# The first product of a compression MLP: blocks as the stationary operand, or the weights

## The chip, the cores and the metric

The kernel runs on one core of a Trainium2 chip. The metric is the time of one execution on the device in microseconds (us). The engines are TensorE (PE in the rows, with its weight loads as PEld), VectorE (DVE), ScalarE (ACT), GpSimd (POOL) and SyncE (SP, which issues DMAs). Each has its own queue and waits on semaphores.

## The reference, cut to what matters

The model has a first block of two layers and a second block of two layers, on 256 tokens of width 1024. The change sits in the second block, in the branch with block-compressed attention. There the keys and the values of two groups are cut into 15 overlapping blocks of 32 tokens, and a small MLP turns every block into one key or value:

```python
NC = 15                                      # blocks of 32 tokens, 16 apart; G = 2 groups, hd = 64
blocks = concatenate([t_s[:, j:j + NC] for j in range(2)], axis=2) + pos_emb
flat = blocks.reshape(B, NC, G, 32 * 64)
return jax.nn.gelu(flat @ w1) @ w2           # w1: 2048 x 256, w2: 256 x 64

k_cmp = _compress(kc, pos_k, wk1, wk2)
v_cmp = _compress(vc, pos_v, wv1, wv2)
s_cmp = einsum('bsghd,bcgd->bghsc', q, k_cmp)     # scores against the 15 compressed keys
```

So the first product is, for keys and for values each, a 30 x 2048 matrix (2 groups x 15 blocks) times a 2048 x 256 one. Two other kinds of attention, over selected and over windowed keys, need nothing of it.

## The kernel before, in words

`second_layers` runs the two layers of the second block in one loop. Each engine has its program written out by hand, and semaphores (`E("name")`) tie them together. `PJ` and `TP` are pairs of PSUM banks that are used in a fixed order of named uses: `fill` waits until the bank's use before last was emptied, `full` marks it filled.

The attention is a loop over k with 12 groups (`GROUPS2`): groups 0 to 3 over selected keys, 4 to 7 over windowed keys, 8 to 11 over compressed keys. The first two of each four have 128 keys, the others 256; the compressed ones 128. In step k TensorE does the scores of group k (`scores`, L1276), then a share of the compression's first product (`compress`, L1238), then the transposes of the probabilities of group k-1 (`turn_p`, L1286) and the products with the values of group k-2 (`values`, L1297). VectorE adds the mask and takes the maximum of group k (L1702, L1902), scales the output of group k-2 (`output`, L1804 to L1816), and after it does one further piece of work from a table `with_group`: `keys_normalised` in step 3 (a reciprocal, L1859), `gelu_in` in step 5, `gelu_out` in step 6. ScalarE does the exponentials (L1587) and the copies out of PSUM (L1582). The scores of a group wait until VectorE has read those of the group before (`sc_read`).

`compress` works through 32 pieces of the contraction, 16 for keys and 16 for values, 7 in each of the steps 0 to 3 and 4 in step 4. A piece is one product: `BLK` (128 x 30, one column per block) stands in the array, and 256 columns of weights stream past it, from the slots `W.raw` into which they were loaded. The result has the 30 blocks on partitions. `gelu_in` copies it out and works on 30 x 512 elements, ScalarE takes the sigmoid (L1573), `gelu_out` multiplies. In step 7, ahead of the scores, TensorE turns the result by four transposes (`hidden`, L1249), VectorE copies it into `HID` (L1823), and `compressed` (L1257, L1262) makes the second product.

All this is in fp32. A product in fp32 leaves two records in the profile, a transpose one: 7 products are x14 in its rows.

Of the kernel before, what the change touches and what calls it, by code (L numbers as in the profile page):

```python
# [6 lines left out]
P = 128  # L7
# [970 lines left out]
def second_layers(nc, chip, A, layers=DEPTH):  # L978
    ctx = Scope()
    with ctx:  # L980
# [32 lines left out]


        HID = H[:, :, RV:RV + HALF].rearrange("p k (f n) -> p k f n", f=2)
        ge = [KP[:, 0:2, :], KP[:, 2:4, :], BP[:, :, :]]
        kcT = H[:, 0, 0:S].rearrange("p (g n) -> p g n", g=2)
        vcp = H[:, 1, 0:P].rearrange("p (g n) -> p g n", g=2)
        part_out = H[:, 0, S:2 * S]
# [83 lines left out]

        tp = [("x", i) for i in range(4)] + [("f", i) for i in range(9)] + [("mv",), ("mw",), ("ma",), ("mg",), ("mz",)]
        tp += [("q", i) for i in range(2)] + [("d", i) for i in range(4)] + [("kn",)]
        tp += [("o", a) for a in range(5)] + [("hd",), ("kc",), ("vc",)]
        tp += [("o", a) for a in range(5, len(GROUPS2))]
        tp += [("bn",), ("kp", 0), ("kp", 1), ("ba", 0), ("ba", 1), ("vt",), ("W",), ("Q",)]
        tp += [("n", 0), ("n", 1)] + [(k, i) for i in range(2) for k in ("U", "I", "D")] + [("Y", 0)]
# [17 lines left out]
        def E(name):  # L1127
            if name not in ev:
                ev[name] = Count(ctx, nc, "e_" + name)
            return ev[name]  # L1130
# [14 lines left out]
        with nc.Fori(0, layers) as l:  # L1145
          with nc.Block() as block:
# [16 lines left out]
            def _(pe):  # L1163
# [65 lines left out]
                def compress(kv, i):  # L1229
                    s = ("cmp", kv)  # L1230
                    b = PJ.fill(pe, (s, 0)) if i == 0 else PJ.aps[PJ.at[(s, 0)] % 2]
                    if i == 0:
                        pe.wait_ge(E("blk").sem, kv + 1)
                    item = W.first[s] + i // 4
                    if i % 4 == 0:
                        W.wait_landed(pe, item)
                    slot = W.raw(item).rearrange("p c (i f) -> p (c i) f", i=2)
                    ins = pe.matmul(b[0:2 * NC, 0:S], BLK[:, kv, i, :], slot[:, i % 4, :], start=(i == 0), stop=(i == 15))  # L1238
                    if i in (3, 7, 11):
                        ins.then_inc(W.used.sem, 1)  # L1240
                    if i == 15:
                        PJ.full(ins)

                def hidden():

                    b = TP.fill(pe, ("hd",))
                    pe.wait_ge(E("gelu").sem, 1)
                    for n in range(4):
                        ins = pe.transpose(b[:, n * 2 * NC:(n + 1) * 2 * NC], ge[0][0:2 * NC, n // 2, (n % 2) * P:(n % 2) * P + P],  # L1249
                                           chip.ident[0:2 * NC, 0:2 * NC])  # L1250
                    TP.full(ins)

                def compressed():
                    b = TP.fill(pe, ("kc",))
                    TP.taken(pe, ("hd",))
                    for f in range(2):
                        ins = pe.matmul(b[:, 0:2 * P], w2k[:, f, :], HID[:, 0, f, :], start=(f == 0), stop=(f == 1))  # L1257
                    TP.full(ins)
                    b = TP.fill(pe, ("vc",))
                    for g in range(2):  # L1260
                        for f in range(2):
                            ins = pe.matmul(b[:, g * HD:(g + 1) * HD], HID[:, 1, f, g * P:(g + 1) * P], w2v[:, f, :],  # L1262
                                            start=(f == 0), stop=(f == 1))
                    TP.full(ins)
# [38 lines left out]
                for k in range(G + 2):  # L1303
                    if k == 2:
                        b = TP.fill(pe, ("kn",))
                        pe.wait_ge(E("ksq").sem, 1)
                        TP.full(pe.matmul(b[:, :], chip.ones[:], TM2.rearrange("p c s -> p (c s)"), start=True, stop=True))
                    if k == 7:
                        hidden()
                    if k < G:  # L1310
                        scores(k)
                    for n in range(7 * k, min(7 * k + 7, 32)):
                        compress(n // 16, n % 16)
                    if 0 <= k - 1 < G:
                        turn_p(k - 1)
                    if k == 7:
                        compressed()
                    if 0 <= k - 2 < G:
                        values(k - 2)
# [175 lines left out]
            def _(act):  # L1495
# [65 lines left out]
                for a in range(G + 1):  # L1561
                    if a == 0:

                        act.wait_ge(E("cum").sem, 1)
                        lane.done(sc.activation(EP[:, :, :], CUM[:, :, :], ACT.Exp), E("exps"))
                        lane.done(sc.activation(EE[:, :, :], EE[:, :, :], ACT.Exp), E("exps"))
                    if a == 1:
                        lane.done(sc.activation(EN[:, :, :], CUM[:, 2:4, :], ACT.Exp, scale=-1.0), E("exps"))
                        lane.done(sc.activation(EM[:, :, :], EM[:, :, :], ACT.Exp), E("exps"))
                    if a == 6:  # L1570

                        act.wait_ge(E("ge_in").sem, 1)
                        lane.done(sc.activation(ge[2][0:2 * NC], ge[1][0:2 * NC], ACT.Sigmoid, scale=2.0 * 0.7978845608028654), E("ge_sig"))  # L1573
                    if a == 2:
                        b = TP.read(act, ("kn",))
                        TP.empty(lane, sc.activation(TM, both(b), ACT.Sqrt), ("kn",))
                    if a >= 1:
                        act.wait_ge(E("pt_full").sem, a)
                        if a - 1 >= 2:
                            act.wait_ge(TP.filled.sem, TP.at[("o", a - 3)] + 1)  # L1580
                        n = keys(a - 1) // P
                        lane.done(sc.copy(PT[:, (a - 1) % 2, 0:n, :], ptb[:, 0:n, :]), E("pt"))  # L1582
                    if a < G:
                        act.wait_ge(E("mx").sem, a + 1)
                        for s in range(4):
                            p = sm[:, a % 2, s, 0:keys(a)]
                            lane.done(sc.activation(p, p, ACT.Exp, bias=nmx[:, a, s:s + 1], accum_out=den[:, a, s:s + 1]),  # L1587
                                      E("p") if s == 3 else None)
# [95 lines left out]
            def _(dve):  # L1684
# [132 lines left out]

                Kn, Rn = FT[:, F_K:F_K + 2, :], FT[:, F_R:F_R + 2, :]

                def hidden():  # L1820
                    b = TP.read(dve, ("hd",))
                    for kv in range(2):
                        ins = v.tensor_copy(HID[:, kv, :, :].rearrange("p f (g n) -> p f g n", g=2)[:, :, :, 0:NC],  # L1823
                                            b[:, kv * 4 * NC:(kv + 1) * 4 * NC].rearrange("p (f g n) -> p f g n", f=2, g=2))
                        lane.done(ins) if kv == 0 else TP.empty(lane, ins, ("hd",))

                def compressed():
                    b = TP.read(dve, ("kc",))
                    TP.empty(lane, v.tensor_copy(H[:, 0, 0:S], b[:, 0:2 * P]), ("kc",))
# [8 lines left out]
                    stt(Kn, BB[:, :, :], 1.0, Kn, ALU.add, ALU.mult)  # L1838


                blocks = slice(0, 2 * NC)

                def gelu_in():
                    for kv in range(2):
                        b = PJ.read(dve, (("cmp", kv), 0))
                        PJ.empty(lane, v.tensor_copy(ge[0][blocks, kv, :], b[blocks, 0:S]), (("cmp", kv), 0))
                    tt(ge[1][blocks], ge[0][blocks], ge[0][blocks], ALU.mult)
                    ts(ge[1][blocks], ge[1][blocks], 0.044715, 1.0, ALU.mult, ALU.add)
                    tt(ge[1][blocks], ge[1][blocks], ge[0][blocks], ALU.mult, E("ge_in"))

                def gelu_out():
                    dve.wait_ge(E("ge_sig").sem, 1)
                    tt(ge[0][blocks], ge[0][blocks], ge[2][blocks], ALU.mult, E("gelu"))

                def keys_normalised():
                    TP.drained(dve, ("kn",))
# [29 lines left out]
                G = len(GROUPS2)  # L1886
                dve.wait_ge(E("gate").sem, 1)
                for k in range(G + 2):
                    if k == 7:
                        hidden()  # L1890
                    if k < G:
                        kind, t, g = GROUPS2[k]
                        nk = keys(k)
                        dve.wait_ge(E("sc_full").sem, k + 1)
                        if k >= 2:

                            dve.wait_ge(E("pt_full").sem, k - 1)
                        p = sm[:, k % 2, :, 0:nk]
                        bias = (chip.cmpb if kind == "c" else chip.cbias)[:, t, 0:nk].unsqueeze(1).to_broadcast([P, 4, nk])
                        stt(p, scb[:, :, 0:nk], 0.125, bias, ALU.mult, ALU.add, E("sc_read"))  # L1900
                        lane.settle()
                        lane.done(v.tensor_reduce(nmx[:, k, :], p, AX_X, ALU.max, negate=True), E("mx"))  # L1902
                    if k == 7:
                        compressed()
                    if k - 2 >= 0:
                        output(k - 2)
                    if k in with_group:
                        with_group[k]()
# [322 lines left out]
```

## Time and profile before

| | us |
|---|---|
| median of three runs | 1833.7 |
| lowest and highest run | 1832.84, 1835.09 |
| span of the profiled execution (first to last instruction) | 1835.8 |
| TensorE busy in it, weight loads aside | 1599.5 |
| VectorE, ScalarE, GpSimd busy | 785.5, 778.1, 968.8 |

The profiled execution is one more execution, apart from the three; of it the profile gives the span. The granted clock is the share of TensorE's full clock of 2.4 GHz that the chip allows; it has two levels, 1.00 and 0.50 (1.2 GHz), and a value between them is a mean over a stretch in which it changed. The steps of the attention stand in the profile at 864 to 950 us (first layer of the second block) and at 1403 to 1488 us (second).

### The profile page before, as it was taken

To read this page: it belongs to the slowest core of one execution; us is meant where nothing else is said; L and a number is where in the kernel's file an instruction comes from. 1 tells how busy PE (TensorE), PEld (TensorE's weight loads), DVE (VectorE), ACT (ScalarE), POOL (GpSimd) and SP (SyncE) were. 2 spreads that over 40 slices of the span, in tenths; PEclk is the share of its full clock that TensorE was granted. 3 is DMA by queue.
4 is the path that set the end of the run, shared out by engine and by line. 5 is a ranking of instruction groups with operands and counts; after the bars stand their busy time and mean duration, and the time that the engine had idled before them with its cause. 6 is when DMAs were issued, how large, how long until landed. Compare 5 with 4: busy or idle time off the path is not lost. (4 is left out here: it accounts for less than half of the span.)

```text
span 1835.8 us, 22140 instructions
## 1 busy us (share of the span) xinstructions
PE 1599.5 (87%) x8104; PEld 1309.1 (71%) x8104; DVE 785.5 (43%) x1135; ACT 778.1 (42%) x1233; POOL 968.8 (53%) x416
## 2 busy tenths in 40 slices
PE   5998999969989999797878789999797868889997
PEld 3876787758867877575568668887575658767885
DVE  5106853541068535108676461111127685551112
ACT  4443664334436643355531234443355522234442
POOL 4785457748854587472000339877670000358875
PEclk8999999989999999797868889999798869789999
DMA  5564335445633354551200326654651100336553
GB/s 165 160 199 121 92 110 160 155 123 162 195 115 92 113 164 146 174 174 51 92 1 1 115 69 190 181 163 144 184 155 61 58 1 22 94 104 193 167 179 125
DMA packets 120671, 228.17 MB, mean 124 GB/s; under 512 B 9968, under 2 KB 22896, under 8 KB 120560
## 3 DMA queue, kind: packets, MB, share of 16 engines
q1 hardware_dynamic: 119408, 222.51, 40.9%
q10 hardware_dynamic: 1152, 4.19, 0.8%
q8 instruction: 68, 1.11, 0.3%
q14 instruction: 43, 0.35, 0.1%
HBM read 225.63 MB, written 1.05 MB: 123 GB/s over the span
## 5 line engine op out<-in xcount | busy, mean ns | idle before, releaser
L162 POOL TENSOR_TENSOR parts<-raw,parts 128x1024 fp32r<-128x1024 f32 (+4 forms) x412 | 968.6, 2362 | 848.6 <-ACT parts L155 846.6
L193 PE MATMUL ps<-parts,xT 128*128 128x512 f32 (+3 forms) x2624 | 812.3, 390 | 24.3 <-ACT xT L1645 7.0
L155 ACT CAST parts<-raw 128x1024 fp32r<-128x1024 f32 (+4 forms) x412 | 417.1, 1015 | 506.7 <-PE ps L193 277.7
L193 PEld LDWEIGHTS ps<-parts,xT 128*128 128x128 f32 x2624 | 496.0, 192 | 134.0 <-ACT xT L1645 7.9
L193 PE MATMUL ps<-parts,x_low 128*128 128x512 f32 (+2 forms) x672 | 255.4, 389 | 0.0
L193 PE MATMUL ps<-parts,M_low 128*128 128x512 f32 (+2 forms) x640 | 244.9, 387 | 0.0
L193 PEld LDWEIGHTS ps<-parts,x_low 128*128 128x128 f32 x672 | 131.1, 195 | 25.2
L193 PEld LDWEIGHTS ps<-parts,M_low 128*128 128x128 f32 x640 | 120.9, 189 | 21.2
L193 PE MATMUL ps<-parts,aT 128*128 128x512 f32 x352 | 109.5, 394 | 0.0
L193 PE MATMUL ps<-parts,H_low 128*128 128x512 f32 x272 | 106.1, 395 | 0.0
L765 DVE TENSOR_TENSOR acc<-H,rope1s 128x512 f32<-128x512 f32 (+1 forms) x6 | 9.6, 1599 | 192.2 <-ACT H L646 192.1
L193 PEld LDWEIGHTS ps<-parts,aT 128*128 128x128 f32 x352 | 66.1, 188 | 15.8 <-POOL parts L162 0.4
L193 PE MATMUL ps<-parts,ysT 128*128 128x512 f32 x192 | 62.7, 399 | 4.9 <-DVE sm L896 4.9
L193 PE MATMUL ps<-parts,mn_high 128*128 128x512 f32 x128 | 47.1, 444 | 21.7 <-ACT parts L155 17.8
L1691 DVE TENSOR_TENSOR DL<-FT 128x2550 f32<-128x2550 f32 x2 | 5.6, 2815 | 128.3 <-ACT FT L1522 128.3
L2098 DVE TENSOR_TENSOR EE<-ps,EE 128x512 f32<-128x512 f32 (+1 forms) x24 | 15.4, 647 | 104.1 <-ACT EE L1671 104.1
L193 PEld LDWEIGHTS ps<-parts,H_low 128*128 128x128 f32 x272 | 51.1, 188 | 11.7
L1362 PE MATMUL ps<-arena 128*128 128x128 f32 x448 | 55.1, 290 | 4.4 <-DVE arena L1967 4.4
L1362 PEld LDWEIGHTS ps<-arena 128*128 128x128 f32 x448 | 54.8, 205 | 5.0 <-DVE arena L1691 5.0
L2105 DVE TENSOR_TENSOR H<-ps,EE 128x512 f32<-128x512 f32 (+1 forms) x24 | 15.5, 647 | 96.7 <-PE ps L193 96.7
L2051 DVE SCALAR_TENSOR_TENSOR x<-x,ps 128x512 f32<-128x512 f32 x16 | 10.9, 682 | 105.5 <-PE ps L193 105.4
L1587 ACT ACTIVATE arena<-arena,nmx 128x128 f32<-128x128 f32 (+1 forms) x96 | 40.7, 426 | 28.4 <-DVE nmx L1902 28.4
(310 smaller groups left out, 2003.5 us busy)
## 6 DMA issues: line engine op xcount, KB each, us to landing
raw<-in_w_in SPq DMA_DIRECT2D x168, 512.0 KB, 3.6
raw<-in_ffn_w_down SPq DMA_DIRECT2D x44, 512.0 KB, 4.2
raw<-in_ffn_w_gate SPq DMA_DIRECT2D x40, 512.0 KB, 3.8
raw<-in_ffn_w_up SPq DMA_DIRECT2D x40, 512.0 KB, 4.4
raw<-in_w_out SPq DMA_DIRECT2D x32, 512.0 KB, 3.8
raw<-in_w_branch SPq DMA_DIRECT2D x24, 512.0 KB, 4.3
raw<-in_w_mem_kv SPq DMA_DIRECT2D x16, 512.0 KB, 3.9
raw<-in_w_in SPq DMA_DIRECT2D x16, 366.0 KB, 3.2
```

Source lines behind the costliest of these rows:

```text
L155: self.nc.scalar.copy(self.part(i, 0)[:, 0:nk, 0:w], self.raw(i)[:, 0:nk, 0:w]).then_inc(self.hi_ready.sem, 1)
L162: self.nc.gpsimd.tensor_tensor(self.part(i, 1)[:, 0:nk, 0:w], self.raw(i)[:, 0:nk, 0:w], self.part(i, 0)[:, 0:nk, 0:w], ALU.subtract).then ...
L193: ins = pe.matmul(b[:, 0:w], a(k0 + 2 * n + c, t), self.part(i, lo_w)[:, c, 0:w], start=(opens and n == p == 0), stop=(final and p == len( ...
L765: lane.done(v.tensor_tensor(a_, X[:, :, :, 0:16], C.unsqueeze(2).to_broadcast([P, NT, nh, 16]), ALU.mult))
L1362: ins = pe.matmul(b[:, u, :], L[:, 4 * par + u, :], R[:, 4 * par + u, :], start=True, stop=True)
L1587: lane.done(sc.activation(p, p, ACT.Exp, bias=nmx[:, a, s:s + 1], accum_out=den[:, a, s:s + 1]), E("p") if s == 3 else None)
L1691: lane.done(v.tensor_tensor(out, a, b, op), e)
L2051: banks.empty(lane, v.scalar_tensor_tensor(out=xs, in0=xs, scalar=ALPHA, in1=b[:, :], op0=ALU.mult, op1=ALU.add), ((s, j), t))
L2098: PJ.empty(lane, v.tensor_tensor(sg[:, t, 0:w], b[:, 0:w], sg[:, t, 0:w], ALU.mult), (("gt", j), t))
L2105: ins = v.tensor_tensor(H[:, t, c0:c0 + w], b[:, 0:w], sg[:, t, 0:w], ALU.mult)
```

## The change: what it does

The weights are now the stationary operand and the blocks stream. A piece takes two products, one for each half of the 256 features: 128 x 128 weights stand, 30 columns of `BLK` stream. The result comes out with the features on partitions, 60 columns for keys and 60 for values. The four transposes and the two copies of `hidden` are gone, with their use ("hd",) of `TP`; `gelu_in`, the sigmoid and `gelu_out` work on 128 x 120 elements in place of 30 x 512, and `gelu_out` writes `HID` itself, in two instructions.

```diff
-        ge = [KP[:, 0:2, :], KP[:, 2:4, :], BP[:, :, :]]
+        ge = [u[:, 0, 0:8 * NC].rearrange("p (k n) -> p k n", k=2) for u in (KP, KP[:, 2:4], BP)]
...
-                    ins = pe.matmul(b[0:2 * NC, 0:S], BLK[:, kv, i, :], slot[:, i % 4, :], start=(i == 0), stop=(i == 15))
+                    for f in range(2):
+                        ins = pe.matmul(b[:, f * 2 * NC:(f + 1) * 2 * NC], slot[:, i % 4, f * P:(f + 1) * P], BLK[:, kv, i, :],
+                                        start=(i == f == 0), stop=(i == 15 and f == 1))
...
-                def hidden():
-
-                    b = TP.fill(pe, ("hd",))
-                    pe.wait_ge(E("gelu").sem, 1)
-                    for n in range(4):
-                        ins = pe.transpose(b[:, n * 2 * NC:(n + 1) * 2 * NC], ge[0][0:2 * NC, n // 2, (n % 2) * P:(n % 2) * P + P],
-                                           chip.ident[0:2 * NC, 0:2 * NC])
-                    TP.full(ins)
-
                 def compressed():
                     b = TP.fill(pe, ("kc",))
-                    TP.taken(pe, ("hd",))
+                    pe.wait_ge(E("gelu").sem, 2)
...
-                    if k == 7:
-                        hidden()
...
                 def gelu_out():
                     dve.wait_ge(E("ge_sig").sem, 1)
-                    tt(ge[0][blocks], ge[0][blocks], ge[2][blocks], ALU.mult, E("gelu"))
+                    for kv in range(2):
+                        tt(HID[:, kv, :, :].rearrange("p f (g n) -> p f g n", g=2)[:, :, :, 0:NC],
+                           ge[0][:, kv, :].rearrange("p (f g n) -> p f g n", f=2, g=2),
+                           ge[2][:, kv, :].rearrange("p (f g n) -> p f g n", f=2, g=2), ALU.mult, E("gelu"))
```

TensorE's order at the start of the loop, steps 0 to 2, before (an "x7" here is 7 products, 14 records of the profile):

```order
L1276 MATMUL ps<-arena 128x128 x4
L1238 MATMUL ps<-raw,arena 30x256 x7
L1276 MATMUL ps<-arena 128x128 x4
L1238 MATMUL ps<-raw,arena 30x256 x7
L1286 MATMUL ps<-ident,arena 128x128 x4
L1307 MATMUL ps<-DL,ones 128x512
L1276 MATMUL ps<-arena 128x256 x4
```

The same place now (L1239 is the compression's product, L1269 the scores, L1279 the transposes):

```order
L1269 MATMUL ps<-arena 128x128 x4
L1239 MATMUL ps<-arena,raw 128x30 x14
L1269 MATMUL ps<-arena 128x128 x4
L1239 MATMUL ps<-arena,raw 128x30 x14
L1279 MATMUL ps<-ident,arena 128x128 x4
L1300 MATMUL ps<-DL,ones 128x512
L1269 MATMUL ps<-arena 128x256 x4
```

Each run of 7 products with 256 streaming columns has become one of 14 with 30; the work around it stands as it did.

TensorE's order in steps 6 and 7 before, from the scores of group 6 to the second product:

```order
L1276 MATMUL ps<-arena 128x256 x4
L1286 MATMUL ps<-ident,arena 128x128 x4
L1297 MATMUL ps<-H,arena 128x64 x4
L1249 MATMUL ps<-ident,DL 128x30 x4
L1276 MATMUL ps<-arena 128x256 x4
L1286 MATMUL ps<-ident,arena 128x128 x8
L1257 MATMUL ps<-H,w2k 128x256 x2
L1262 MATMUL ps<-w2v,H 128x64 x4
```

The same place now (L1290 is the product with the values, L1250 and L1255 the second product):

```order
L1269 MATMUL ps<-arena 128x256 x4
L1279 MATMUL ps<-ident,arena 128x128 x4
L1290 MATMUL ps<-H,arena 128x64 x4
L1269 MATMUL ps<-arena 128x256 x4
L1279 MATMUL ps<-ident,arena 128x128 x8
L1250 MATMUL ps<-H,w2k 128x256 x2
L1255 MATMUL ps<-w2v,H 128x64 x4
```

The four transposes ahead of the scores of group 7 are gone; the wait for the activated result has moved behind the transposes of group 6.

## Rows read from the trace of the kernel before

**Rows 1.** The page: time, TensorE's busy time, granted clock in 40 slices.

```profile
span 1835.8 us, 22140 instructions
...
PE 1599.5 (87%) x8104; PEld 1309.1 (71%) x8104; DVE 785.5 (43%) x1135; ACT 778.1 (42%) x1233; POOL 968.8 (53%) x416
...
PEclk8999999989999999797868889999798869789999
```

**Rows 2.** Chain that ended last, second layer: start us, us, what.

```profile
1416.04 3.14 PE ps L1238 x14
...
1433.79 3.36 DVE DL L1859
```

**Rows 3.** Timeline of TensorE, first layer, steps 0 to 7: start us, us busy.

```profile
870.53 5.65 PE L1238 MATMUL ps<-raw,arena 128*30 128x256 f32 x14 [4.93 <-issue]
876.11 0.71 PE L1276 MATMUL ps<-arena 64*128 64x128 f32 x8
...
880.39 1.02 PE L1307 MATMUL ps<-DL,ones 128*128 128x512 f32 x2
881.34 1.13 PE L1276 MATMUL ps<-arena 64*128 64x256 f32 x8
...
893.04 0.71 PE L1276 MATMUL ps<-arena 64*128 64x128 f32 x8
...
914.04 0.60 PE L1249 MATMUL ps<-ident,DL 30*128 30x30 f32 x4 [4.02 <-DVE DL L1691]
```

**Rows 4.** Stretches: us, busy us (instructions) of PE, PEld, DVE, ACT, POOL, PEclk, DMA, GB/s.

```profile
870.53:875.50 4.97, 4.97 (x12) 2.08 (x13) 3.52 (x6) 1.08 (x6) 0.00 (x0) 0.50 0.06 11
...
876.10:893.10 17.00, 17.00 (x103) 10.10 (x102) 8.25 (x12) 9.75 (x24) 0.00 (x0) 1.00 0.56 178
...
1052.50:1060.00 7.50, 7.50 (x34) 7.28 (x34) 3.69 (x9) 2.07 (x3) 0.00 (x0) 0.50 0.02 3
```

**Rows 5.** Groups of TensorE's instructions in 1052.5 to 1060 us.

```profile
L1420 PE MATMUL ps<-H,arena 128*128 128x64 f32 x8 | 2.5, 421 | 0.0
```

**Rows 6.** Timeline of TensorE, second layer, steps 4 to 9.

```profile
1438.75 1.23 PE L1276 MATMUL ps<-arena 64*128 64x128 f32 x8 [1.18 <-DVE arena L1702]
1441.15 1.11 PE L1286 MATMUL ps<-ident,arena 128*128 128x128 f32 x4 [1.18 <-ACT arena L1587]
1442.06 3.52 PE L1297 MATMUL ps<-H,arena 128*128 128x64 f32 x16
1445.50 2.08 PE L1276 MATMUL ps<-arena 64*128 64x256 f32 x8
...
1454.58 2.08 PE L1276 MATMUL ps<-arena 64*128 64x256 f32 x8
1456.59 1.97 PE L1286 MATMUL ps<-ident,arena 128*128 128x128 f32 x8
1458.35 1.46 PE L1257 MATMUL ps<-H,w2k 128*128 128x256 f32 x4
...
1463.05 1.90 PE L1297 MATMUL ps<-H,arena 128*128 128x64 f32 x16
1464.88 0.72 PE L1276 MATMUL ps<-H,arena 64*128 64x128 f32 x8
```

**Rows 7.** Timeline of VectorE, first layer, steps 4 to 7.

```profile
900.34 0.18 DVE L1804 RECIPROCAL fac<-den 128x4 f32<-128x4 f32 x1
...
906.35 0.73 DVE L1846 COPY DL<-ps 30x256 f32<-30x256 f32 x2
...
909.20 1.23 DVE L1702 SCALAR_TENSOR_TENSOR arena<-ps,cbias 128x1024 f32<-128x1024 f32 x1
...
913.21 0.68 DVE L1691 TENSOR_TENSOR DL<-DL,BP 30x512 f32<-30x512 f32 x1
914.68 0.35 DVE L1823 COPY H<-ps 128x60 f32<-128x60 f32 x2 [0.79 <-PE ps L1249]
916.70 1.22 DVE L1702 SCALAR_TENSOR_TENSOR arena<-ps,cbias 128x1024 f32<-128x1024 f32 x1 [1.67 <-PE ps L1276]
```

More of the change, by code:

```diff
@@ L1105, in second_layers @@
         tp += [("q", i) for i in range(2)] + [("d", i) for i in range(4)] + [("kn",)]
-        tp += [("o", a) for a in range(5)] + [("hd",), ("kc",), ("vc",)]
+        tp += [("o", a) for a in range(5)] + [("kc",), ("vc",)]
         tp += [("o", a) for a in range(5, len(GROUPS2))]
@@ L1572, in _ @@
                         act.wait_ge(E("ge_in").sem, 1)
-                        lane.done(sc.activation(ge[2][0:2 * NC], ge[1][0:2 * NC], ACT.Sigmoid, scale=2.0 * 0.7978845608028654), E("ge_sig"))
+                        lane.done(sc.activation(ge[2], ge[1], ACT.Sigmoid, scale=2.0 * 0.7978845608028654), E("ge_sig"))
                     if a == 2:
@@ L1818, in _ @@
                 Kn, Rn = FT[:, F_K:F_K + 2, :], FT[:, F_R:F_R + 2, :]
[L1820 to L1825, printed above, removed]
                 def compressed():
@@ L1838, in keys_mixed @@
                     stt(Kn, BB[:, :, :], 1.0, Kn, ALU.add, ALU.mult)
-                blocks = slice(0, 2 * NC)
                 def gelu_in():
@@ L1845, in gelu_in @@
                         b = PJ.read(dve, (("cmp", kv), 0))
[L1846 to L1849, printed above, removed]
+                        PJ.empty(lane, v.tensor_copy(ge[0][:, kv, :], b[:, 0:4 * NC]), (("cmp", kv), 0))
+                    tt(ge[1], ge[0], ge[0], ALU.mult)
+                    ts(ge[1], ge[1], 0.044715, 1.0, ALU.mult, ALU.add)
+                    tt(ge[1], ge[1], ge[0], ALU.mult, E("ge_in"))
                 def gelu_out():
                     dve.wait_ge(E("ge_sig").sem, 1)
-                    tt(ge[0][blocks], ge[0][blocks], ge[2][blocks], ALU.mult, E("gelu"))
+                    for kv in range(2):
+                        tt(HID[:, kv, :, :].rearrange("p f (g n) -> p f g n", g=2)[:, :, :, 0:NC],
+                           ge[0][:, kv, :].rearrange("p (f g n) -> p f g n", f=2, g=2),
+                           ge[2][:, kv, :].rearrange("p (f g n) -> p f g n", f=2, g=2), ALU.mult, E("gelu"))
                 def keys_normalised():
@@ L1888, in _ @@
                 for k in range(G + 2):
-                    if k == 7:
-                        hidden()
                     if k < G:
```

## The prediction

> **What bounds the kernel now.** I read the page first. TensorE is busy for 1599.5 us of the span, and in the slices around 870 to 950 us and 1400 to 1490 us its granted clock dips [rows 1]. These are the attention steps of the two layers, the only place that the change touches. The chain that ended last says what the end waits for there: in steps 0 to 3 it stays on TensorE, with the 14 records of a share of the compression as its largest piece, 3.14 us, and in step 4 it passes over to VectorE at the reciprocal of 3.36 us [rows 2]. From there to the end of the loop it goes through the cycle of mask, exponential, transposes and values. So steps 0 to 3 are worth what TensorE takes for them, and later steps are worth the waits between engines.
>
> The timeline of TensorE gives the lengths. The compression's first share starts at 870.53, the scores of group 1 at 876.11, and the scores of group 4, the end of step 3, at 893.04, with no gap [rows 3]. The stretches give the clock: 0.50 from 870.5 to 875.5, then 1.00 for the whole of 876.1 to 893.1, with TensorE busy for 17.00 of 17.00 us [rows 4]. Before the rise TensorE had done twelve records with 256 streaming columns. That clock of 1.00 is the thing to watch: every piece in steps 1 to 4 is short because of it.
>
> **The change part by part.**
>
> *The compression's product.* 64 records per layer with 256 streaming columns become 128 with 30 columns, each with 128 columns of weights to load. The trace has no product with 30 streaming columns. The nearest is the values' product: 128 columns loaded, 64 streaming. At the full clock 16 of its records take 1464.88 - 1463.05 = 1.83 us, 0.114 each; at 0.50, 1445.50 - 1442.06 = 3.44 us, 0.215 each [rows 6]. A record with 256 columns takes 3.14 / 14 = 0.224 at the full clock [rows 2], so a stream of 64 columns should take a quarter, 0.056. The record costs twice that: the weight load sets it, and fewer columns make it no cheaper. I take 0.114 and 0.215. A share of 28 records is then 3.20 us at the full clock (before 3.14) and 6.02 at 0.50 (before 5.58, which included the first records after the rise) [rows 2, 3]. The other bound is that load and stream lie one after the other: 0.114 = 0.058 + 0.056, and 30 columns would make 0.058 + 0.026 = 0.084, or 0.16 at 0.50. That would take 0.03 x 128 = 3.8 us per layer off at the full clock, 7 us at 0.50.
>
> So at equal clock the product costs the same as before. The multiplications fall out of it, the loads come in.
>
> *The clock.* This decides. Where TensorE worked through records of 128 loaded and 64 streaming columns it did not get its full clock however busy it was: from 1052.5 to 1060 us it was busy for 7.50 of 7.50 us, and the clock stood at 0.50 throughout [rows 4]; 24 of the 34 records there are of three such lines, 8 each, of which one row is shown [rows 5]. The 3.44 us of the values at 1442.06 are such a stretch too, and the scores behind them still run slowly (2.01 us) [rows 6]. The new shares stream half as many columns per load. In step 0 the engine starts at 0.50, so nothing there should lift it, and in steps 1 to 4 they are the largest piece. I take 0.50 for steps 0 to 4.
>
> The price of the other pieces at 0.50: scores with 128 keys 1.2 us (busy time 1.23), with 256 keys 1456.59 - 1454.58 = 2.01; four transposes 1442.06 - 1441.15 = 0.91, eight 1458.35 - 1456.59 = 1.76; values with 16 records 3.44, so 1.72 with 8 [rows 6]; the product with `ones` twice 881.34 - 880.39, 1.9 [rows 3].
>
> - step 0: compression 6.0
> - step 1: 1.2 + 6.0 + 0.9 = 8.1
> - step 2: 1.9 + 2.0 + 6.0 + 0.9 + 1.7 = 12.5
> - step 3: 2.0 + 6.0 + 1.8 + 1.7 = 11.5
>
> Together 38.1 us in place of 893.04 - 870.53 = 22.5: **+15.6 us**. In step 4 TensorE then needs 1.2 + 3.4 (16 records) + 1.8 + 3.4 = 9.8 us until the values of group 2 are there, at about 918.5. VectorE took up their output at 900.34 [rows 7], held by the reciprocal, which hid TensorE's step; at 0.50 it no longer does. The delay grows to about **+18.2 us**. Steps 5 to 7 are at 0.50 before as well, mostly, and carry it on.
>
> *What is given back.* `gelu_in` took 909.20 - 906.35 = 2.85 us on 512 elements per partition. A copy of 60 takes 0.35 / 2 = 0.18 [rows 7]; with two such copies and three operations on 120 at about 0.3 with their waits, it takes some 1.5: **-1.3**. From `gelu_out` to the mask of group 7 VectorE took 916.70 - 913.21 = 3.49 us [rows 7]: the multiplication, the wait for TensorE's transposes, the copies, and the wait for the scores of group 7, which stood behind them, while TensorE idled 4.02 us for the result [rows 3]. Now the scores of group 7 are done in this idle time and VectorE goes on after two products of 60 elements, some 0.5 us: **-3.0**. The wait for the activated result moves behind the transposes of group 6. Behind it are queued the second product and the values of group 5, for which VectorE waits; `gelu_out` is done about when the exponentials of group 6 are, so it adds nothing. The shorter sigmoid is a part of ScalarE's waiting. The second product is unchanged.
>
> Per layer: 18.2 - 4.3 = +13.9 us with the clock at 0.50 throughout. It may rise in between, where `ones`, 256-key scores and transposes stand together. These pieces of steps 2 and 3 are 6.5 + 5.5 = 12 us at 0.50; all of them at 1.00 would save 6, and a share that followed at 1.00 another 2.8. I take 1.5 off, as a choice between 0 and 9. So +12.4 per layer, **+25 for two**: the profiled execution of 1835.8 becomes 1861, and the median, 2.1 below it, **1858**.
>
> A rule speaks against this sum. The Trainium skill (TensorE: Matmul & The Clock Gate, section "Why this matters for your kernels") asks for one thing for the full rate, that TensorE is kept busy without a break; by that the new shares would raise the clock as the old did. The trace contradicts it at 1052.5 to 1060 us, busy throughout at 0.50 [rows 4].
>
> **The rivals.**
>
> *The clock rises all the same and stays up: faster.* The place is the end of step 0. For it speaks that TensorE is busy without a gap in steps 0 to 3, as before, and that the full clock, once there, survives 1.83 us of values records in a row [rows 6]. Against it: 7.50 us at 0.50 [rows 4]. Then the shares cost 3.20 for 3.14, +0.3 us per layer with step 4, and the 4.3 us come back whole: -4.0 per layer, -8 in all, **1826**. It turns where the delay of steps 0 to 4 is under 4.3 us per layer, that is where TensorE is at 0.50 for less than some 9 of its 22 us after step 0. By the page's rule above it would come out like this.
>
> *The load is cheaper than I take it, the clock low.* By the other bound above, 7 us per layer less: +5.4 per layer, about **1845**.
>
> *The clock is not lifted anywhere and stays low in steps 8 to 11 as well*, which before ran partly at 1.00: some 5 us more per layer on top of the 13.9, **1871**.
>
> *Both effects cancel*: the clock is up for about half of steps 1 to 4, and the delay is about 4 us: **1834**, no change.
>
> **How the numbers follow.** The forecast, clock at 0.50 for most of steps 0 to 4, from +8 to +15 per layer (1850 to 1864), has 0.66. The cheaper load has 0.07, the clock low to the end 0.09, cancelling 0.04, and the clock up 0.14. The cases on the slow side sum to 0.82. The range leaves out the clock that stays up and the cancelling, 0.18: from 1838, a cheap load with some rises, to 1874, a little above the rival with the low clock. A measurement tells this kernel from no change at about 0.2%, 3.7 us: faster 0.14, within it 0.04, slower 0.82.
>
> **What the changed profile would show.** The granted clock in the stretches of steps 1 to 4: near 0.50 by the forecast, 1.00 by the first rival. A share of the compression as x28 in about 6.0 us, or 3.2. The time from its first record to the scores of group 4: 38 us, or 22.6. VectorE's output of group 2 waiting for TensorE. In step 7 no wait of 4 us ahead of the scores, and some 1.5 us for `gelu_in`. A record of the new product well under 0.114 at the full clock, or under 0.215 at half, would refute the load as its price. The forecast is wrong if the clock column stays at 1.00; nothing else in it is large enough to turn the sign.

## The result, and the profile after

The changed kernel takes 1852.25 us in the median of five runs (1844.17 to 1857.63), the kernel before 1833.7 in the median of five (1827.09 to 1837.12). The ratio is 1.0095, with an interval of 1.0068 to 1.0123: slower by some 18 us, where 25 were forecast. The profiled execution of the changed kernel has a span of 1848.1 us, 12.3 above that of before.

The page of the changed kernel, in the lines that answer to [rows 1], and one group of its part 5:

```profile
span 1848.1 us, 22374 instructions
...
PE 1626.6 (88%) x8224; PEld 1352.8 (73%) x8224; DVE 780.7 (42%) x1133; ACT 777.4 (42%) x1233; POOL 968.6 (52%) x416
...
PEclk9999999989999999797669789999896659889999
...
L1239 PE MATMUL ps<-arena,raw 128*128 128x30 f32 x256 | 50.9, 372 | 9.9 <-issue 9.9
```

TensorE's busy time is up by 27 us, and the clock is lower in the slices around 900 us and from 1390 to 1480 us. The busy time of the group is no measure of its cost, since records overlap; starts are. The timeline of TensorE in the second layer (start us, us busy), the answer to [rows 3]:

```profile
1410.80 6.15 PE L1239 MATMUL ps<-arena,raw 128*128 128x30 f32 x28 [4.93 <-issue]
1416.88 1.23 PE L1269 MATMUL ps<-arena 64*128 64x128 f32 x8
...
1428.77 6.18 PE L1239 MATMUL ps<-arena,raw 128*128 128x30 f32 x28
...
1448.87 1.23 PE L1269 MATMUL ps<-arena 64*128 64x128 f32 x8
...
1458.64 1.23 PE L1269 MATMUL ps<-arena 64*128 64x128 f32 x8
```

And in the first layer:

```profile
870.63 6.15 PE L1239 MATMUL ps<-arena,raw 128*128 128x30 f32 x28 [4.93 <-issue]
...
877.87 6.18 PE L1239 MATMUL ps<-arena,raw 128*128 128x30 f32 x28
883.86 1.09 PE L1279 MATMUL ps<-ident,arena 128*128 128x128 f32 x4
...
887.74 3.31 PE L1239 MATMUL ps<-arena,raw 128*128 128x30 f32 x28
890.89 0.64 PE L1279 MATMUL ps<-ident,arena 128*128 128x128 f32 x4
...
899.49 1.23 PE L1269 MATMUL ps<-arena 64*128 64x128 f32 x8
```

The same share of 28 records stands here at both prices: 883.86 - 877.87 = 5.99 us, and 890.89 - 887.74 = 3.15 us. Which one it gets is told by the stretches of the changed kernel (columns as in [rows 4]):

```profile
870.63:886.80 16.17, 16.17 (x72) 14.38 (x74) 6.12 (x11) 4.49 (x18) 0.00 (x0) 0.50 0.33 98
886.90:897.00 10.10, 10.10 (x89) 9.28 (x88) 5.66 (x7) 6.04 (x14) 0.00 (x0) 1.00 0.39 116
897.10:899.49 2.39, 2.39 (x13) 2.27 (x11) 0.00 (x0) 1.49 (x4) 0.00 (x0) 0.50 0.76 253
1410.80:1448.87 38.07, 38.07 (x170) 34.40 (x171) 11.77 (x18) 12.13 (x35) 0.00 (x0) 0.50 0.33 97
```

TensorE is busy without a pause in all four. In the second layer the clock is 0.50 for the whole of steps 0 to 3, which take 38.07 us. In the first layer it rises at 886.8 us, in the scores of group 2 right behind the product with `ones`, and stays up for 10 us; the same steps take 899.49 - 870.63 = 28.86 us.

VectorE in steps 5 to 7 of the first layer, the answer to [rows 7]:

```profile
915.64 0.34 DVE L1828 COPY DL<-ps 128x60 f32<-128x60 f32 x2
...
917.11 1.23 DVE L1693 SCALAR_TENSOR_TENSOR arena<-ps,cbias 128x1024 f32<-128x1024 f32 x1
...
921.12 0.47 DVE L1682 TENSOR_TENSOR H<-DL,BP 128x60 f32<-128x60 f32 x2
921.73 1.23 DVE L1693 SCALAR_TENSOR_TENSOR arena<-ps,cbias 128x1024 f32<-128x1024 f32 x1
```

`gelu_in` takes 1.47 us (2.85 before), and from `gelu_out` to the mask of group 7 there are 0.61 us (3.49 before).

### The profile page after: what moved, and what is told of

The parts are those of the page before. It is cut to its first block and busy times, and to the rows that moved or that the text cites. A ratio compares the mean times of both kernels' runs of the same rounds, so it can differ in the third digit from the quotient of the medians.

```text
span 1848.1 us, 22374 instructions
## 1 busy us (share of the span) xinstructions
PE 1626.6 (88%) x8224; PEld 1352.8 (73%) x8224; DVE 780.7 (42%) x1133; ACT 777.4 (42%) x1233; POOL 968.6 (52%) x416
## 5 line engine op out<-in xcount | busy, mean ns | idle before, releaser
L193 PE MATMUL ps<-parts,mn_high 128*128 128x512 f32 x128 | 47.1, 445 | 20.2 <-ACT parts L155 18.2
L1239 PE MATMUL ps<-arena,raw 128*128 128x30 f32 x256 | 50.9, 372 | 9.9 <-issue 9.9
L1239 PEld LDWEIGHTS ps<-arena,raw 128*128 128x128 f32 x256 | 49.7, 301 | 13.2 <-issue 13.2
```

The costliest lines, as they stand in the source:

```text
L193: ins = pe.matmul(b[:, 0:w], a(k0 + 2 * n + c, t), self.part(i, lo_w)[:, c, 0:w], start=(opens and n == p == 0), stop=(final and p == len( ...
L1239: ins = pe.matmul(b[:, f * 2 * NC:(f + 1) * 2 * NC], slot[:, i % 4, f * P:(f + 1) * P], BLK[:, kv, i, :], start=(i == f == 0), stop=(i == ...
```

## The experiments

All were timed against the kernel before on the same chip; e1 to e4, e5 to e8 and e9 to e11 had a chip per group, so between the groups the ratios are what compares. To compare profiles, the attention loop of each layer is measured from the first scores of group 0 to the product with `ones` behind the loop; before that is 945.96 - 864.38 = 81.58 us and 1485.62 - 1403.51 = 82.11. The whole execution also moves by what the clock does elsewhere: 29 runs of the kernel before lay between 1817.94 and 1842.21, and of the 17.3 us by which the span of e1 is below that of before, 8.1 lie in the two loops. A loop in this table is one profile's.

| kernel | median us | ratio (interval) | loop, layers one and two, against before |
|---|---|---|---|
| changed | 1852.25 | 1.0095 (1.0068 to 1.0123) | +3.8, +12.5 |
| changed, again (e4) | 1853.57 | 1.0110 (1.0071 to 1.0149) | +13.2, +12.7 |
| 120 columns (e1) | 1822.77 | 0.9953 (0.9929 to 0.9977) | -5.1, -3.0 |
| 60 columns (e2) | 1830.81 | 0.9985 (0.9962 to 1.0007) | +1.1, +1.5 |
| before, transposes moved (e3) | 1840.01 | 1.0030 (1.0009 to 1.0052) | +3.6, +2.7 |
| changed, warmed (e5) | 1840.39 | 1.0028 (1.0004 to 1.0052) | +7.7, +8.7 |
| 120 columns, warmed (e6) | 1821.01 | 0.9936 (0.9915 to 0.9957) | -3.9, -6.0 |
| 120 columns, early wait (e7) | 1821.63 | 0.9941 (0.9914 to 0.9968) | -2.8, -2.4 |
| before, warmed (e8) | 1832.41 | 0.9993 (0.9974 to 1.0012) | 0.0, -0.1 |
| 120 columns, values 128 (e9) | 1824.04 | 0.9939 (0.9918 to 0.9959) | -0.9, -3.8 |
| changed, values 128 (e10) | 1835.52 | 1.0019 (0.9999 to 1.0039) | +6.5, +3.1 |
| before, values 128 (e11) | 1833.00 | 0.9992 (0.9972 to 1.0013) | +0.3, -0.1 |

**More streaming columns behind the same loads (e1, e2).** With c = 4 or c = 2 copies of the 30 columns:

```diff
-                        ins = pe.matmul(b[:, f * 2 * NC:(f + 1) * 2 * NC], slot[:, i % 4, f * P:(f + 1) * P], BLK[:, kv, i, :],
-                                        start=(i == f == 0), stop=(i == 15 and f == 1))
+                        ins = pe.matmul(b[:, f * c * 2 * NC:(f + 1) * c * 2 * NC].rearrange("p (r n) -> p r n", r=c), slot[:, i % 4, f * P:(f + 1) * P],
+                                        BLK[:, kv, i, :].unsqueeze(1).to_broadcast([P, c, 2 * NC]), start=(i == f == 0), stop=(i == 15 and f == 1))
...
```

VectorE's copies in `gelu_in` read the first copy of the columns only.

> The changed kernel, but each of its 64 products streams the same 30 block columns four times over, 120 columns in all, into four places of the bank, of which one is read. Loads, number of records, everything behind them and the result stay as they are in the changed kernel; only the streaming columns per load change. Theory (the low clock in steps 0 to 4 is the loss, and it stands low because TensorE mostly loads): the clock rises after step 0 and stays at 1.00 through steps 1 to 4, a share of 28 records takes 3.2 us, and only what the change gives back remains: 4.0 us per layer under the kernel before, about 1826 us. Rival (the loss is in the records themselves, in loads that add to the stream or in their number): a record with four times the columns takes at least as long as now, 0.215 us, and the time is that of the changed kernel, 1852 us, or more.

> As the kernel with 120 streaming columns, but the 30 columns are streamed twice, 60 columns per load, which is the shape nearest to the values' product with its 64. Theory: stretches of such records stood at 0.50 in the kernel before (1052.5 to 1060 us), so the shares alone don't lift the clock, but the pieces between them do so more often than in the changed kernel: between the two, 1835 to 1850 us. Rival (the clock follows how long TensorE is busy, whatever it does): 1852 us, as changed. Rival (the records themselves): 1852 us or more.

With 120 columns the kernel takes 1822.77 us: 30 us less than the changed kernel, for streaming four times as much. The timeline of TensorE and a stretch of it:

```profile
870.34 3.38 PE L1239 MATMUL ps<-arena,raw 128*128 128x120 f32 x28
873.56 0.60 PE L1279 MATMUL ps<-ident,arena 128*128 128x128 f32 x4
...
886.70 0.72 PE L1269 MATMUL ps<-arena 64*128 64x128 f32 x8
```

```profile
868.60:886.70 18.10, 18.10 (x153) 16.22 (x151) 8.25 (x12) 11.18 (x32) 0.00 (x0) 1.00 0.58 176
```

A share takes 873.56 - 870.34 = 3.22 us, against 3.15 for 30 columns at the same clock, and the clock is 1.00 from the rise in step 0 to the end of step 3. The theory stands, and its rival, that the records themselves are the loss, falls: longer records, and a faster kernel. What remains is the give-back, -5.1 and -3.0 us in the loops, where -4.0 per layer was forecast.

With 60 columns I expected 1835 to 1850 and measured 1830.81. The timeline shows why this is better than expected:

```profile
869.93 6.20 PE L1239 MATMUL ps<-arena,raw 128*128 128x60 f32 x28 [4.93 <-issue]
...
877.22 6.23 PE L1239 MATMUL ps<-arena,raw 128*128 128x60 f32 x28
...
886.78 3.33 PE L1239 MATMUL ps<-arena,raw 128*128 128x60 f32 x28
889.95 0.61 PE L1279 MATMUL ps<-ident,arena 128*128 128x128 f32 x4
...
892.39 3.34 PE L1239 MATMUL ps<-arena,raw 128*128 128x60 f32 x28
```

Two shares in a row stay at the low clock, as the records of 64 columns did at 1052.5 to 1060 us [rows 4]. Then it rises, in the product with `ones` here (at some 885.4 us) and in the scores of group 2 in the other layer, and with these shares it stays; from 885.5 to 898 us it is 1.00. With shares of 30 columns it fell again in the changed kernel, at 897.0 us, after two of them. So a shape with which the clock does not rise can still be one with which it stays.

**The changed kernel a second time (e4).**

> The changed kernel once more, unaltered, for a second profile. In the first one the clock stood at 0.50 through steps 0 to 4 of the second layer, but rose from 886.8 to 897.1 us in the first, where the delay to the end of the loop was 3.8 us in place of 12.5. Theory (whether the clock rises between the shares hangs on how the pieces fall against the chip's own grid): the second profile has another pattern of rises, in either layer, and the runs spread over 1842 to 1860 us as before. Rival (the first layer has something of its own that lifts the clock, such as the transfers): the same pattern again, up in the first layer and low in the second.

The time is confirmed, 1853.57 us, and the pattern is another one: both layers at 0.50 through steps 0 to 3. The stretches:

```profile
868.40:906.38 37.98, 37.98 (x170) 34.31 (x170) 11.69 (x18) 12.13 (x35) 0.00 (x0) 0.50 0.32 96
1421.20:1459.30 38.10, 38.10 (x172) 34.43 (x172) 11.78 (x18) 12.16 (x35) 0.00 (x0) 0.50 0.32 97
```

The first layer's +3.8 us in the first profile is therefore no property of that layer. That execution had a rise between the shares, this one has none before step 4 (there, in the product with the values, the clock rises in both layers), and its span is 1860.9 us. What decides it I did not vary: that it hangs on how the pieces fall against a grid of the chip, as the expectation has it, stays an assumption.

**The order alone (e3).**

```diff
-                    if k == 7:
-                        hidden()
                     if k < G:
                         scores(k)
...
                     if k == 7:
+                        hidden()
                         compressed()
...
```

> The kernel before, with its product as it was, and only the four transposes of the MLP's result moved: from ahead of the scores of group 7 to behind the transposes of group 6, and VectorE's copies with them, to behind the mask and maximum of group 7. This is the part of the give-back that is order alone. Theory: scores and mask of group 7 no longer wait for the result; of the 3.0 us that the removal of the transposes gives in step 7, some 2 remain per layer, 1829 to 1831 us. Rival (the wait only moves, since the second product and the values of group 5 now stand behind it): 1833.7 us.

This went the other way, 0.3% slower, and neither theory had it. TensorE in steps 6 to 8:

```profile
914.69 1.97 PE L1286 MATMUL ps<-ident,arena 128*128 128x128 f32 x8 [2.23 <-ACT arena L1586]
916.59 0.63 PE L1249 MATMUL ps<-ident,DL 30*128 30x30 f32 x4
917.76 2.04 PE L1257 MATMUL ps<-H,w2k 128*128 128x256 f32 x4 [0.53 <-DVE H L1822]
919.60 1.80 PE L1262 MATMUL ps<-w2v,H 128*128 128x64 f32 x8
921.19 1.91 PE L1297 MATMUL ps<-H,arena 128*128 128x64 f32 x8
```

In the kernel before the same two pieces are:

```profile
916.58 1.97 PE L1286 MATMUL ps<-ident,arena 128*128 128x128 f32 x8
...
920.82 1.06 PE L1297 MATMUL ps<-H,arena 128*128 128x64 f32 x8
```

The loop starts at 863.94 us here and at 864.38 before. Counted from there, the transposes of group 6 start at 50.75 us, 1.4 earlier than before (52.20). Then the four transposes and a wait of 0.53 us for VectorE's copies stand on TensorE's path to the second product, and the second product and the values of group 5 run at the low clock: the values start at 57.25 us, before at 56.44. The pieces behind them stay slow to 927.3 us, where before the clock was up from 919.9. So the head start is more than used up. The changed kernel has the same order without transposes and copies. The profiled execution is the slowest of the twelve, so how much of the 0.3% each of the two makes is not shown.

**The wait put back (e7).** The kernel with 120 columns, and in step 7:

```diff
+                    if k == 7:
+                        pe.wait_ge(E("gelu").sem, 2)
                     if k < G:
                         scores(k)
```

> The kernel with 120 streaming columns, but in step 7 TensorE waits for the activated result ahead of the scores of group 7, where the four transposes stood before. Nothing else is changed. It undoes the order part of the give-back at a clock that is up. Theory (what step 7 gives back is the scores and the mask of group 7, freed of the wait): 1.5 to 2.5 us per layer are lost again, 1826 to 1828 us. Rival (the gain in step 7 comes from the missing transposes and copies, and the place of the wait is worth nothing, as the slower run with the transposes moved suggests): 1823 us.

The times do not tell it from e1 (1821.63 and 1822.77), and the loops are only 2.2 and 0.6 us longer; the 1826 to 1828 us that I expected did not come. VectorE shows the local price:

```profile
912.49 0.47 DVE L1684 TENSOR_TENSOR H<-DL,BP 128x60 f32<-128x60 f32 x2
914.73 1.22 DVE L1695 SCALAR_TENSOR_TENSOR arena<-ps,cbias 128x1024 f32<-128x1024 f32 x1 [1.77 <-PE ps L1269]
```

From `gelu_out` to the mask there are 2.24 us, against 3.49 before and 0.61 in the changed kernel. Of the 2.9 us that step 7 gives back, the place of the wait is 1.6 in this layer, and transposes, copies and the shorter multiplication are 1.3; in the other layer the split is 2.0 and 0.9. The scores behind the wait took 1.67 us in this layer, against 1.13 in the changed kernel, so the clock that was up in steps 1 to 4 was not up here. What the wait is worth in the time stays open, since it is less than a measurement tells.

**A raised clock to begin with (e5, e6, e8).** In step 0, ahead of the first share:

```diff
+                    if k == 0:
+                        for _ in range(5):
+                            pe.matmul(ptb[:, 0, :], chip.ones[:], chip.masks[:, 0:4, :].rearrange("p a n -> p (a n)"), start=True, stop=True)
```

> The changed kernel, and in the 4.9 us in which TensorE waits for the block columns in step 0 it does five idle products of 128 x 512 (constants, into a bank that is free), whose result nobody reads. They bring the full clock to the first share, and shares of 30 columns follow. Theory (shares of 30 streaming columns don't hold the full clock): part of share 0 runs at 1.00, some 2 to 3 us per layer less, then the clock falls again during share 0 or 1 and stands at 0.50 in most of steps 1 to 4; 1845 to 1851 us beside the changed kernel's 1853. Rival (a clock once up survives such records, as it did 1.83 us of values' products): 1.00 through steps 0 to 4, as with 120 columns and 3 us per layer better, 1817 us.

> The same five idle products, ahead of the shares with 120 streaming columns. Theory (step 0 runs at 0.50 only because TensorE stood idle before it, and its 6.0 us are on the path): share 0 takes 3.2 to 4.5 us in place of 6.0, 1.5 to 2.8 us per layer, so 1817 to 1820 us beside 1823 without them. Rival (what step 0 saves is lost again, since VectorE's masks and ScalarE's exponentials of group 0 then are what step 1 waits for): 1823 us.

> The kernel before with the five idle products ahead of its first share. Theory (as for 120 columns): share 0 drops from 5.6 to 3.1 to 4.2 us, 1.4 to 2.5 us per layer, 1829 to 1832 us. Rival: the clock falls earlier in steps 5 to 7 by as much as it rises earlier, no change against the kernel before.

In steps 0 and 1 e5 did what the theory says. Its timeline and stretches:

```profile
863.58 6.07 PE L1305 MATMUL ps<-masks,ones 128*128 128x512 f32 x10
869.49 3.21 PE L1239 MATMUL ps<-arena,raw 128*128 128x30 f32 x28
872.62 0.72 PE L1269 MATMUL ps<-arena 64*128 64x128 f32 x8
873.26 6.01 PE L1239 MATMUL ps<-arena,raw 128*128 128x30 f32 x28
...
883.80 3.31 PE L1239 MATMUL ps<-arena,raw 128*128 128x30 f32 x28
886.95 0.95 PE L1279 MATMUL ps<-ident,arena 128*128 128x128 f32 x4
```

```profile
869.49:873.40 3.91, 3.91 (x39) 3.75 (x37) 2.73 (x6) 0.86 (x5) 0.00 (x0) 1.00 0.24 46
873.60:883.60 10.00, 10.00 (x41) 7.90 (x40) 2.38 (x5) 4.99 (x16) 0.00 (x0) 0.50 0.42 138
```

Share 0 runs at 1.00 and takes 3.13 us; the clock then falls, with TensorE busy throughout, and share 1 takes 5.83. The rival, that a clock once up survives such records, is refuted. The time, 1840.39 us, is below the 1845 to 1851 that I expected, although the warming has a price that the expectations left out. The idle products take longer than the wait of 4.93 us, so share 0 starts 7.07 and 6.88 us behind the first scores in the two layers, in the changed kernel 6.15. At its end 2.0 and 2.2 us are left, 4.2 of the 13 by which e5 is faster. More came from share 2, which ran at 1.00 in both layers: 886.95 - 883.80 = 3.15 us, and 3.15 in the second, 2.8 less each than at 0.50. Whether the warm start brings these later rises, one profile does not tell.

At the full clock the warming gives little: 1821.01 against 1822.77 (e6) and a ratio of 0.9993 for the kernel before (e8), whose loops are as long as without it. Share 0 starts 1.0 to 1.5 us later there as well. In the first layer of e8 it still ends 1.2 us ahead of before; then the clock falls earlier (the transposes of group 4 take 1.11 us, before 0.66), and the scores of group 8 start at 57.40 us from the first scores, before at 57.43. So e8 went to its rival.

**The same trick on the values' product (e9, e10, e11).**

```diff
-                            ins = pe.matmul(b[:, s * HD:(s + 1) * HD], PT[:, a % 2, kt, s * P:(s + 1) * P], v,
+                            ins = pe.matmul(b[:, s * P:(s + 1) * P].rearrange("p (r d) -> p r d", r=2), PT[:, a % 2, kt, s * P:(s + 1) * P],
+                                            v.unsqueeze(1).to_broadcast([P, 2, HD]),
```

> The kernel with 120 streaming columns in the compression, and the same done to the values' product of the attention loop: its 64 columns are streamed twice, 128 per load, into twice as many columns of the bank, of which VectorE reads the first copy. The result is the same. Theory (a record that loads 128 columns costs its load, 0.114 us at the full clock, up to 128 streaming columns, and what streams behind the load keeps the clock up): values' records at 1.00 take no longer, and the clock is up in more of steps 4 to 11, 1 to 3 us per layer less: 1816 to 1821 us beside 1822.8. Rival (in steps 5 to 11 TensorE idles for VectorE and ScalarE, and the clock there follows the pauses): no change, 1823 us. Rival (the record gets longer by its stream): slower than 1823.

> The changed kernel, 30 streaming columns in the compression, with only the values' 64 columns streamed twice. It asks whether the pieces between the shares lift the clock enough. Theory: steps 2 to 4 have rises more often, since the values' records stream as many columns as they load; 1838 to 1848 us beside 1853. Rival (the shares alone decide): 1853 us.

> The kernel before with only the values' 64 columns streamed twice. Theory: steps 0 to 4 have the full clock already, so only steps 4 to 11 can gain, 1 to 3 us per layer: 1828 to 1832 us. Rival (pauses decide there): 1834 us. If this gains as much as it does on top of the kernel with 120 columns, the two effects add.

On the changed kernel it takes 18 us off (1835.52 for 1853.57; by the ratios, 17), more than the 5 to 15 expected, although the compression is untouched. On the kernel with 120 columns and on the one before it gives nothing, where 1 to 3 us per layer were expected: 1824.04 and a ratio of 0.9992. There steps 1 to 4 have the full clock already, and the rival is what the times agree with. Where the 18 us of e10 arise its profile tells in part only. TensorE in the second layer:

```profile
1422.61 1.62 PE L1269 MATMUL ps<-arena 64*128 64x256 f32 x8
...
1428.44 1.92 PE L1290 MATMUL ps<-H,arena 128*128 128x128 f32 x8
1430.28 1.20 PE L1269 MATMUL ps<-arena 64*128 64x256 f32 x8
```

The clock rises first at 1423.5 us, in the scores of group 2 and so ahead of the loop's first product with the values, as it did in the changed kernel; it falls, rises again at 1430.3 right behind that product, and then stays at 1.00 to 1448. In the first layer it stood at 0.50 to 894.5 us and was at 1.00 from 901.5 to 942.3, so part of the gain lies behind the shares. That the pieces between the thin shares count for the clock is shown by the time; that they bring the rises in steps 0 to 3 is not.

## Why the prediction was right, and where it was off

*What bounds it.* Steps 0 to 3 are worth what TensorE takes for them. Right: every stretch of them above is filled, and where the delay was +18.7 at step 4 the loop still ended 12.5 later.

*The price of a record.* Forecast 0.114 and 0.215 us. Measured 3.15 / 28 = 0.1125 and 5.99 / 28 = 0.214. The other bound, load and stream one after the other, 0.084, is refuted twice: by 30 columns, and by 120, whose share takes 3.22 us (0.115 per record). At equal clock the product costs what it cost before, as said.

*The clock.* The decisive step, right: steps 0 to 3 took 38.07 us at 0.50 in three of four layers profiled (in e4 the stretches are cut at 37.98 and 38.10), where the sum gave 38.1. That the low clock is the loss, and not only beside it, is shown by e1: the same loads, the same number of records, the clock at 1.00, and the loss gone.

*The rises in between.* Here the sum was mis-sized: "I take 1.5 off, as a choice between 0 and 9". One layer of four took off 38.1 - 28.86 = 9.2, the other three nothing. With +18.6 in the medians instead of the 27.8 at 0.50 throughout, they are worth about 4.6 us per layer in the mean, if all the rest is as forecast, and 3.5 with the +12.8 us per layer that the layers without a rise in steps 0 to 3 measured. The two profiles show a layer either with a rise worth 9 us or with none, not a small saving in each; of the other runs there is no trace. That 1852 came so near to 1858 is in part luck, since the 1.5 was a choice.

*The delay at step 4.* Forecast +18.2. In the second layer the scores of group 5, which before waited 1.18 us for VectorE and now do not wait, start 1458.64 - 1410.80 = 47.8 us behind the first share, before 1438.75 - 1409.66 = 29.1: +18.7. In e4, where the clock rose in step 4, it was +18.1 and +18.0. The line of before that [rows 6] does not have:

```profile
1409.66 5.74 PE L1238 MATMUL ps<-raw,arena 128*30 128x256 f32 x14 [4.93 <-issue]
```

*What is given back.* Forecast -1.3 and -3.0, measured 1.47 - 2.85 = -1.4 and 0.61 - 3.49 = -2.9. The reason given for the second, only the order, was too simple: e3 has the order and is slower, e7 lacks it and isn't measurably so.

*The layer as a whole.* +13.9 forecast for the low clock, measured +12.5, +12.7 and +13.2. The +18.7 at step 4 and the -4.3 of the give-back leave +14.4 in the second layer, and the loop ends at +12.5. Behind step 5 the clock was up for longer there, from 1467.1 to 1484.1 us where before it was up from 1459.3 to 1472.8, which the forecast did not count; that this is the whole difference is argued, not shown.

The rivals: the clock that stays up (1826) did not come, but e1 built it, and 1822.8 is near its price. The cheaper load is refuted. The low clock to the end (1871) did not come: it was 1.00 from 1467.1 to 1484.1 us. Nor did the cancelling (1834). The rule of the Trainium skill cited there (TensorE: Matmul & The Clock Gate, section "Why this matters for your kernels"), that TensorE need only be kept busy, is contradicted here: it was busy for 38.07 of 38.07 us, and the clock stood at 0.50.

**The better version.** The kernel with 120 columns beats both, 0.9953 (0.9929 to 0.9977) of the time before; with the idle products 0.9936 (0.9915 to 0.9957), which is not told apart from it.

## What to carry to other kernels

When an operand is swapped, price the load and the stream of each record apart, and then ask what the new mix of loads and streams does to the clock of its neighbours; here the product kept its price at either clock and the stretch around it cost up to 16 us more per layer. A thin product behind a full weight load can stream its columns several times over and take hardly longer (3.22 us for 3.15 here, with four times the columns), and that can be what keeps the clock. In a profile, read the granted clock of the stretch before its busy time, and of a kernel with such stretches take a second profile.

## What the runs showed of the hardware

- A record that loads 128 fp32 columns costs 0.1125, 0.113 and 0.115 us with 30, 60 and 120 streaming columns at the full clock (28 records in 3.15, 3.17 and 3.22 us; the middle one is 889.95 - 886.78), and 0.214 at half: the cost of the load goes with the clock.
- The clock stood at 0.50 with TensorE busy for 38.07 us in steps 0 to 3, and in the second layer of the first profile on to 1466.9 us, 56.1 us in all. It did not rise in two shares of 60 columns per load, and stayed up in the next ones (e2); with 30 it fell, some 4 us into them in e5, and in the changed kernel after 10 us with other pieces between.
- The rises in steps 2 and 3 beside such shares (changed kernel, e2, e5, e10) lie in the product with `ones` or in scores with 256 keys, or right behind them.
- One kernel, two profiles, 1848.1 and 1860.9 us: 9.3 of the 12.8 lie in the loop of the layer in which the clock rose.
